# Order of the first projections in an encoder layer on one core: values of two attention units first, per token tile

## The chip, the cores and the metric

The kernel runs on one core of one Trainium2 chip. The metric is device microseconds of the whole program on that core; the time of a kernel is the median of its runs. Each engine (TensorE or PE, VectorE or DVE, ScalarE or ACT, GpSimd or POOL, SyncE or SP, which only issues transfers here) executes its own instructions strictly in program order and waits on semaphores where the kernel says so.

## What is computed

One layer of an encoder over 512 tokens of width 1024, in float32: a normalised input, one wide projection into queries, keys and values of three kinds of attention, the attentions, a gated mix, and a feed-forward part. The change touches only the first lines:

```python
u = rmsnorm(h, g_pre_mix[i])
proj = u @ w_in[i]
qa, ka, va, qb, kb, vb, qc, kc, vc = jnp.split(proj, SPLIT_POINTS, axis=-1)
...
ya = diff_attention(qa..., ka..., va..., t5_table[:, :A_HEADS], lam, lam_init, subln_g[i])
```

## The kernel before, in words

Every float32 product is done as three products of parts: an operand is split into a high part (a cast copy, by ACT) and a low part (the source less the high part, by DVE for activations, by POOL for weights), and `triple` multiplies high by high, high by low and low by high into the same bank of PSUM. The normalised and transposed input lies in `u_hi` and `u_lo` (128 features x 8 x 512 tokens). Weights come in tiles of 128 columns (1024 x 128), in a ring of `RING` = 4 slots: SP loads a tile into `raw`, ACT casts it into `whi` (`w_hi`, L1014), POOL makes `wlo` in four pieces (`w_lo`, L856), and then the tile is ready for PE.

The order of the projections is written out in `attention_gemms`. It gives a list of tiles (`TILES`: q, k and v of unit 0, then q, k and v of each next unit, and tiles of the gate late), and a list of steps (`STEPS`: one step is one k of one tile, three matmuls of 512 columns). Attention has 12 units (four of kind A, four C, four B) of four slots each (one for 128 queries); `STEPS[-1]` is the head, before the first slot, and `STEPS[s]` are the steps that PE does in slot s, while ACT and DVE work on the softmax. In a slot PE does its steps, then `pv(s - 1)`, `qk(s + 1)` and `turn_probs(s)` (transposes of the probabilities). `FINISH[t]` is the slot in which a tile is complete. A finished q or k tile is taken out of its bank in two stages: ACT copies the high part (`proj_out`; L1066 for q, L1075 for k), then DVE makes the low part (`proj_low`; L1641 for q, L1647 for k). A v tile has features on the partitions, so ACT copies it to `v_feat` (L1086), PE turns it back in four transposes at the unit's first slot (`turn_v`, L2376), ACT copies the high part (L1178) and DVE makes the low part (L1824). `bank_free` holds PE back before a tile until the bank's former tile is out.

The head, in order. The input comes in four token tiles x(0) to x(3). ACT sums the squares (`square`, L1024), POOL makes the reciprocal root (`rstd`, L866), DVE scales (L1581 in halves for tiles 0 and 1, L1563 for tiles 2 and 3), PE transposes (L2320, L2299), ACT copies the high part (L1041, L1028), DVE makes the low part (L1587, L1569). A matmul of ones (L2313) spreads the gain over the partitions. `keep_clock_up` issues transposes of the identity that compute nothing (L2307). Then PE multiplies q and k of unit 0 over token tiles 0 and 1 (weights stationary, 256 columns), with tiles 2 and 3 of the input transposed between and the small tables turned by `turn_tables` (L2288 to L2293), then over tiles 2 and 3, then v of unit 0 over all 512 tokens, and then `qk(0)` (L2364, L2365), which waits until q and k of unit 0 are out (`proj_lo`). DVE meanwhile runs `tables()` (L1597 to L1621): it copies the turned tables, makes the bias by distance in 29 copies, and waits for the mask. After it DVE takes up `proj_low` of the first tiles, in order of tiles. ACT stores the bias table to DRAM, from which SP loads the bias of each head.

Of the kernel before, what the change touches and what calls it, by code (L numbers as in the profile page):

```python
# [41 lines left out]
SLOT_CUTS = {"A": (0, 5, 11, 17, 24), "C": (0, 5, 10, 16, 24), "B": (0, 6, 11, 17, 24)}  # L42
WARM_UP = (14, 2, 6)
# [79 lines left out]
def attention_gemms():  # L123


    tiles, steps = [], {-1: []}
    for kind in "qkv":
        steps[-1] += [(len(tiles), k) for k in range(KT)]
        tiles.append((kind, 0))
    gate = 0  # L130
    for u in range(UNITS):
        mine = []
        if u + 1 <= 8:
            mine = [("q", u + 1), ("k", u + 1), ("v", u + 1)]
            if u + 1 == 8:
                mine[:2] = mine[1::-1]
        elif u + 1 < UNITS:
            mine = [("gate", gate), ("q", u + 1), ("gate", gate + 1)]
            gate += 2
        else:  # L140
            mine = [("gate", gate), ("gate", gate + 1)]
        flat = [(len(tiles) + i, k) for i in range(len(mine)) for k in range(KT)]
        tiles += mine
        cuts = SLOT_CUTS[branch(u)] if len(flat) == 3 * KT else [len(flat) * qt // TT for qt in range(TT + 1)]
        for qt in range(TT):
            steps[4 * u + qt] = flat[cuts[qt]:cuts[qt + 1]]
    finish = {t: s for s, st in steps.items() for t, k in st if k == KT - 1}
    return tiles, steps, finish
# [6 lines left out]
def split_slot(t):  # L155

    return -1 if t < RING else FINISH[t - RING] + 1
# [15 lines left out]
def build_encoder(nc, x, w_in, lambda_q1, lambda_k1, lambda_q2, lambda_k2, subln_g, t5_table, sinks,  # L173
# [16 lines left out]
    with ExitStack() as ctx:  # L190
# [67 lines left out]
        def turned_tokens(t, done):  # L258


            return bank2(TT - 1 - t if done == 0 else t).rearrange("p (k n) -> p k n", n=P)

        def first_turned(part):

            return bank2(TT - 1 - part).rearrange("p (k n) -> p k n", n=2 * P)
# [199 lines left out]
        small_loaded = [sem(f"small_loaded{i}") for i in range(9)]  # L465
# [9 lines left out]
        first_half_hi = sem("first_half_hi")  # L475
        quarter_lo = sem("quarter_lo")
        xs_first = sem("xs_first")
        tile_used = sem("tile_used")
# [154 lines left out]
        def _(sp):  # L633
# [5 lines left out]
            load_x(2)  # L639

            def load_small():
# [3 lines left out]
                sp.dma_start(conv_in[:, 3, :], conv_b[0].rearrange("(j n) -> j n", n=P)).then_inc(small_loaded[4], 16)  # L645
                sp.dma_start(bgate_in, b_gate[0].rearrange("(j n) -> j n", n=P)).then_inc(small_loaded[5], 16)
                for i, v in enumerate((lambda_q1, lambda_k1, lambda_q2, lambda_k2)):
                    sp.dma_start(lam_in[:, i, :], v[0].partition_broadcast(P)).then_inc(small_loaded[7], 16)
                sp.dma_start(sink[:], sinks[0].partition_broadcast(P)).then_inc(small_loaded[6], 16)
                sp.dma_start(sub_raw[:], subln_g[0].rearrange("(n a) -> n a", a=1)).then_inc(small_loaded[8], 16)  # L650
# [10 lines left out]
            def by_k(t, r, src, n=KT):  # L661

                h = n // 2
                load(t, r, (raw_k[:, r, 0:h, :], raw_k[:, r, h:n, :]), (src[:, 0:h, :], src[:, h:n, :]))

# [31 lines left out]
            for u in range(4, UNITS - 1):  # L697
                bias_before[min(t for t in range(2 * RING, T_ATT) if split_slot(t - RING) >= TT * (u - 1))] = u
            for t, (kind, n) in enumerate(TILES):
# [7 lines left out]
                if t == 1:  # L707
                    load_x(3)
# [4 lines left out]
                if kind == "gate":  # L713
                    by_k(t, t % RING, gate_v[:, :, n, :])
                else:
# [3 lines left out]
                    by_k(t, t % RING, win_v[:, :, col:col + P])  # L719
            load_biases(UNITS - 1)  # L720
# [122 lines left out]
        def _(pool):  # L843
# [34 lines left out]
            def w_lo_quarter(t, i):  # L878
                c = slice(256 * i, 256 * (i + 1))
                pool.tensor_tensor(wlo[:, t, c], raw[:, t, c], whi[:, t, c].bitcast(F32), ALU.subtract)\  # L880
                    .then_inc(quarter_lo if i < 3 else w_lo_done, 1)

            rstd(0, 0)
            rstd(0, 1)
            rstd(0, 2)
            pool.wait_ge(first_half_hi, 1)
            w_lo_quarter(0, 0)
            w_lo_quarter(0, 1)
            pool.wait_ge(w_hi_done, 1)
            w_lo_quarter(0, 2)  # L890
            w_lo_quarter(0, 3)
            rstd(0, 3)
            pool.wait_ge(w_hi_done, 2)
            for i in range(4):
                w_lo_quarter(1, i)
# [6 lines left out]
            pool.wait_ge(mask_done, 1)  # L902
            for s in range(SLOTS):
# [106 lines left out]
        def _(act):  # L1010
# [5 lines left out]
            def w_hi_at(t):  # L1016
                if t >= RING:
                    act.wait_ge(tile_used, t - RING + 1)
# [17 lines left out]
            act.wait_ge(x_loaded[2], 16)  # L1036
            square(0, 2, x_tok[:, 2, :])

            def u_high_first(part):
                act.wait_ge(xs_turned, part + 1)  # L1040
                act.copy(u_hi[:, 4 * part:4 * part + 4, 0:2 * P], first_turned(part)).then_inc(u_hi_done, 1)  # L1041

            u_high_first(0)
            act.wait_ge(raw_loaded[0], 32)
            act.copy(whi[:, 0, 0:512], raw[:, 0, 0:512]).then_inc(first_half_hi, 1)
            u_high_first(1)
            act.copy(whi[:, 0, 512:1024], raw[:, 0, 512:1024]).then_inc(w_hi_done, 1)
            act.wait_ge(x_loaded[3], 16)
            square(0, 3, x_tok[:, 3, :])
# [1812 lines left out]
```

## Time and profile before

| | us |
|---|---|
| median of 3 runs | 844.48 (843.78 to 846.26) |
| the profiled execution | 843.84 |
| its span, first to last instruction | 842.0 |
| PE busy in the span | 833.5 (99%) |
| DVE busy | 653.8 (78%) |
| ACT busy | 481.5 (57%) |
| POOL busy | 400.1 (48%) |

The profile gives one execution. The span is 1.84 us shorter than that execution's own time; what lies around it is not in the trace. A PE row of the timeline lists a matmul with a modelled duration that overlaps the next one; the distance from start to start is what a matmul costs in a row of them. The granted clock is 1.00 nearly throughout.

### The profile page before, as it was taken

Reading aid. Unit: us, or ns where it says so; the run is one execution under the profiler, and the core shown is the slowest. Engines: PE = TensorE matmul, PEld = TensorE weight load, DVE = VectorE, ACT = ScalarE, POOL = GpSimd, SP = SyncE. Lnnn points to the kernel's source line nnn. Section 1 sums busy time; section 2 is a strip of 40 time slices with the busy share of each in tenths; the row PEclk is TensorE's granted clock in tenths of the full one; section 3 lists DMA queues with packets and bytes.
Section 4 is the critical chain, followed back from the end, with each engine's and each line's share of the span. In section 5 each row is a group of like instructions: output and inputs, shape, how many; then the busy total and the mean of one; then the engine's idle time right before and its main releaser. Section 6 shows DMA issues by size and latency. Waiting matters only on the chain.

```text
span 842.0 us, 13461 instructions
## 1 busy us (share of the span) xinstructions
PE 833.5 (99%) x4721; PEld 729.3 (87%) x4721; DVE 653.8 (78%) x1257; ACT 481.5 (57%) x906; POOL 400.1 (48%) x511
## 2 busy tenths in 40 slices
PE   8999999999999999999999999999999999999997
PEld 7888888888888888999998889899999999988885
DVE  6678877788866767966544389988888888999996
ACT  6566666777666664544444447456565656545662
POOL 5554443334444446987667435756565656010002
PEclk9999999999999999999999999999999999999999
DMA  8542223233233212333335641555553433396584
GB/s 229 158 121 55 64 86 99 75 98 82 83 82 81 62 41 88 113 110 110 107 101 206 198 147 51 172 175 179 162 178 112 131 110 129 132 329 219 172 285 157
DMA packets 139079, 111.35 MB, mean 132 GB/s; under 512 B 7591, under 2 KB 122223, under 8 KB 137732
## 3 DMA queue, kind: packets, MB, share of 16 engines
q1 hardware_dynamic: 137386, 102.05, 39.8%
q0 software_dynamic: 720, 5.24, 1.7%
q10 hardware_dynamic: 906, 3.20, 1.0%
q8 instruction: 38, 0.62, 0.3%
q14 instruction: 29, 0.24, 0.1%
HBM read 97.05 MB, written 13.42 MB: 131 GB/s over the span
## 4 chain that ended last, share of the span: by engine, by line
PE 94%; DVE 2%; POOL 1%; DMA 1%; ACT 1%; issue 1%; DVEq 0%; SPq 0%; ACTq 0%
PE banks L2280 23%; PE banks L2282 23%; PE banks L2281 23%; PE banks L2557 3%; PE banks L2556 3%; PE banks L2555 3%; PE banks L2456 2%; PE banks L2365 2%; PE banks L2364 2%; PE banks L2726 1%; PE banks L2725 1%; PE banks L2724 1%; PE banks L2428 1%; PE banks L2435 1%; PE banks L2419 1%; DVE scratch L1976 1%
## 5 line engine op out<-in xcount | busy, mean ns | idle before, releaser
L856 POOL TENSOR_TENSOR ring_lo<-ring_raw,ring_hi 128x256 fp32r<-128x256 f32 x376 | 307.2, 850 | 262.8 <-ACT ring_hi L1014 262.4
L2280 PE MATMUL banks<-u_hi,ring_hi 128*128 128x512 f32 (+1 forms) x612 | 231.3, 378 | 0.5 <-POOL ring_lo L880 0.5
L2282 PE MATMUL banks<-u_hi,ring_lo 128*128 128x512 f32 (+1 forms) x612 | 226.4, 370 | 0.0
L2281 PE MATMUL banks<-u_lo,ring_hi 128*128 128x512 f32 (+1 forms) x612 | 226.1, 370 | 0.0
L2282 PEld LDWEIGHTS banks<-u_hi,ring_lo 128*128 128x128 f32 x612 | 115.2, 188 | 20.2
L2280 PEld LDWEIGHTS banks<-u_hi,ring_hi 128*128 128x128 f32 x612 | 115.4, 189 | 18.6 <-DVE u_lo L1587 0.8
L2281 PEld LDWEIGHTS banks<-u_lo,ring_hi 128*128 128x128 f32 x612 | 115.6, 189 | 18.0
L1014 ACT CAST ring_hi<-ring_raw 128x1024 fp32r<-128x1024 f32 x95 | 98.9, 1044 | 37.4 <-PE banks L2282 24.1
L2101 DVE SCALAR_TENSOR_TENSOR wide<-banks,cols,wide 128x511 f32<-128x511 f32 x88 | 64.6, 745 | 3.5 <-ACT wide L1374 1.6
L2280 PE MATMUL banks<-pages,ring_hi 128*128 128x512 f32 (+1 forms) x180 | 61.2, 340 | 0.0
L2281 PE MATMUL banks<-pages,ring_hi 128*128 128x512 f32 (+1 forms) x180 | 61.2, 340 | 0.0
L2282 PE MATMUL banks<-pages,ring_lo 128*128 128x512 f32 (+1 forms) x180 | 61.1, 340 | 0.0
L863 POOL TENSOR_SCALAR norm_ms<-norm_ss 128x1 f32<-128x1 f32 x15 | 6.0, 399 | 100.0 <-ACT pages L1024 99.8
L1162 ACT ACTIVATE scratch<-scratch,negmax 128x193 f32<-128x193 f32 (+5 forms) x96 | 49.4, 517 | 6.7 <-DVE negmax L1752 6.0
L2280 PE MATMUL banks<-ring_hi,pages 128*128 128x512 f32 x112 | 44.0, 393 | 0.0
L2281 PE MATMUL banks<-ring_lo,pages 128*128 128x512 f32 x112 | 43.6, 389 | 0.0
L2282 PE MATMUL banks<-ring_hi,pages 128*128 128x512 f32 x112 | 43.6, 389 | 0.0
L940 POOL TENSOR_TENSOR ring_lo<-ring_raw,ring_hi 128x256 fp32r<-128x256 f32 x44 | 37.6, 874 | 11.7 <-ACT ring_hi L1402 11.7
L1374 ACT ACTIVATE wide<-banks,cols 128x512 f32<-128x512 f32 x40 | 31.0, 775 | 21.1 <-DVE banks L2075 13.4
L1752 DVE CUSTOM_DVE_ANT_0 scratch<-banks,scratch 128x128 f32<-128x128 f32 (+3 forms) x64 | 28.8, 487 | 13.0 <-PE banks L2456 9.1
L2282 PEld LDWEIGHTS banks<-pages,ring_lo 128*128 128x128 f32 x180 | 34.2, 190 | 3.7
L2280 PEld LDWEIGHTS banks<-pages,ring_hi 128*128 128x128 f32 x180 | 34.2, 190 | 3.6
(325 smaller groups left out, 1991.9 us busy)
## 6 DMA issues: line engine op xcount, KB each, us to landing
ring_raw<-in_w_ffn_up_dram SPq DMA_DIRECT2D x88, 256.0 KB, 3.6
ring_raw<-in_w_in_dram SPq DMA_DIRECT2D x60, 256.0 KB, 3.4
ring_raw<-in_w_ffn_down_dram SPq DMA_DIRECT2D x55, 256.0 KB, 3.6
ring_raw<-in_w_gate_dram SPq DMA_DIRECT2D x48, 256.0 KB, 3.2
split_tokens<-pages SPq DMA_DIRECT2D x5, 1024.0 KB, 7.0
pages<-split_tokens POOLq DMA_DIRECT2D x5, 1024.0 KB, 6.5
ring_raw<-in_w_out_dram SPq DMA_DIRECT2D x16, 256.0 KB, 3.1
second_tokens<-wide SPq DMA_DIRECT2D x10, 384.0 KB, 3.9
```

Source lines behind the costliest of these rows:

```text
L856: last = pool.tensor_tensor(wlo[:, r, c], raw[:, r, c], whi[:, r, c].bitcast(F32), ALU.subtract)
L940: last = pool.tensor_tensor(dst[:, c], src[:, c], hi[:, c].bitcast(F32), ALU.subtract)
L1014: act.copy(whi[:, r, :], raw[:, r, :]).then_inc(w_hi_done, 1)
L1162: act.activation(p_out, p_in, ACT.Exp, scale=-1.0, bias=negmax[:, s % 2, m:m + 1], accum_out=rowsum[:, s % 2, m:m + 1]).then_inc(exp_done, 1)
L1374: act.activation(wide[:, 4 + 2 * j + c, :], psum[:, 2 * j + c, :], ACT.Identity, scale=cols[:, 88 + fc:89 + fc], bias=cols[:, 132 + fc:133 ...
L1752: dve.tensor_tensor_reduce(scratch[:, P_PAGE + m, c0:c0 + n], psum[:, SC_BANK + m, 0:n], scratch[:, BIAS_PAGE + b % 4, j0:j0 + n], -1.0, c ...
L2101: dve.scalar_tensor_tensor(out=y[:, back:SEQ], in0=psum[:, 2 * j + c, 0:SEQ - back], scalar=tap, in1=y[:, back:SEQ], op0=ALU.mult, op1=ALU ...
L2280: pe.matmul(out, lhs_hi, rhs_hi, start=start, stop=False)
L2281: pe.matmul(out, lhs_hi, rhs_lo, start=False, stop=False)
L2282: return pe.matmul(out, lhs_lo, rhs_hi, start=False, stop=stop)
L2555: pe.matmul(dst, w_h, u_h, start=False, stop=False, skip_group_check=True)
L2556: pe.matmul(dst, w_h, u_l, start=False, stop=False, skip_group_check=True)
```

## The change

The tiles are in another order. The first two are `va0` and `vb0`: together they are the value weights of units 0 and 1 (256 columns), `va` for k 0 to 3 and `vb` for k 4 to 7. Their products are made by a new function with the tokens as the stationary operand, one token tile after the other, 256 columns moving, so that the values come out with tokens on the partitions. q0 and k0 follow, still in the head; then q1, k1, v2 in unit 0, q2, k2, v3 in unit 1, and so on. The head holds four tiles where it held three; the slots hold 272 steps where they held 280. v of units 0 and 1 is no longer turned. ACT and DVE take `va` and `vb` out of the banks in two pieces of 128 x 256 each. The head's order of token tiles, of splits and of loads changes with it; x(2) and x(3) are issued behind the first two weight tiles. The weight splits of tiles 4 and 5 are done ahead of the slots, and their casts wait until both value tiles are used. The function `first_turned` and the early turns for token tiles 0 and 1 together are gone; twelve fewer empty transposes are issued (28 to 16).

```diff
-SLOT_CUTS = {"A": (0, 5, 11, 17, 24), "C": (0, 5, 10, 16, 24), "B": (0, 6, 11, 17, 24)}
-WARM_UP = (14, 2, 6)
+GEMM_ORDER = ("va0 vb0 q0 k0 q1 k1 v2 q2 k2 v3 q3 k3 v4 q4 k4 v5 q5 k5 v6 q6 k6 v7 q7 k7 v8 k8 q8 "
+              "gate0 q9 gate1 gate2 q10 gate3 gate4 q11 gate5 gate6 gate7")
+SLOT_CUTS = ((0, 5, 11, 17, 23),) + 3 * ((0, 5, 11, 17, 24),) + 4 * ((0, 5, 10, 17, 24),) + (
+    (0, 6, 11, 17, 23), (0, 5, 11, 16, 22), (0, 5, 11, 16, 22), (0, 3, 7, 10, 14))
+SPLIT_AHEAD = RING + 2
+WARM_UP = (11, 4, 1)
...
+    steps, at = {-1: flat[:RING * KT]}, RING * KT
+    for u, cuts in enumerate(SLOT_CUTS):
...
@@ SP
             load_x(0)
             load_x(1)
-            load_x(2)
...
-                if t == 1:
+                if t == 2:
+                    load_x(2)
                     load_x(3)
...
+                elif kind in ("va", "vb"):
+                    by_k_wide(t, t, win_v[:, 4 * t:4 * t + 4, VA:VA + 2 * P])
@@ POOL
             rstd(0, 0)
             rstd(0, 1)
+            w_lo(0, 0)
+            pool.wait_ge(w_hi_done, 2)
+            w_lo_quarter(1, 0)
             rstd(0, 2)
...
+            w_lo_quarter(1, 1)
+            w_lo_quarter(1, 2)
+            w_lo_quarter(1, 3).then_inc(w_lo_done, 1)
             rstd(0, 3)
...
+            for t in range(RING, SPLIT_AHEAD):
+                w_lo(t, t % RING)
@@ ACT
             square(0, 1, x_tok[:, 1, :])
...
+            w_hi_at(0)
+            act.wait_ge(first_turned, 1)
+            act.copy(u_hi[:, 0:4, 0:P], turned_tokens(0, 0)[:, 0:4, :]).then_inc(u_first_hi, 1)
+            act.wait_ge(xs_turned, 1)
+            act.copy(u_hi[:, 4:8, 0:P], turned_tokens(0, 0)[:, 4:8, :]).then_inc(u_hi_done, 1)
+            w_hi_at(1)
+            u_high(1, 0)
             act.wait_ge(x_loaded[3], 16)
+            act.wait_ge(squares, 3)
             square(0, 3, x_tok[:, 3, :])
-            w_hi_at(1)
+            w_hi_at(2)
             u_high(2, 0)
             u_high(3, 0)
-            w_hi_at(2)
             w_hi_at(3)
...
+                elif kind in ("va", "vb"):
+                    for h in range(2):
+                        dst, half = first_values(g, 0, h)
+                        last = act.copy(dst, half)
+                    last.then_inc(proj_act, 1)
...
+            proj_out(0)
             act.wait_ge(lam_dots, 2)
             act.activation(lam_exp[:], lam_dot[:], ACT.Exp).then_inc(lam_exps, 1)
-            proj_out(0)
             proj_out(1)
+            w_hi_at(RING)
             act.wait_ge(dist_done, 2)
             act.dma_start(bias_dram[0:12, :], dist_ab).then_inc(dist_stored, 16)
             act.dma_start(bias_dram[12:20, :], dist_c).then_inc(dist_stored, 16)
+            for t in range(RING + 1, SPLIT_AHEAD):
+                w_hi_at(t)
             proj_out(2)
+            proj_out(3)
@@ DVE
+            xs(0, 1, x_tok[:, 1, :], spread_gain())
             for part in range(2):
...
+                dve.wait_ge(u_hi_done if part else u_first_hi, 1)
+                dve.tensor_tensor(u_lo[:, ks, 0:P], turned_tokens(0, 0)[:, ks, :], u_hi[:, ks, 0:P].bitcast(F32), sub)\
+                   .then_inc(u_lo_done if part else u_first_lo, 1)
+            dve.wait_ge(x_loaded[2], 16)
+            dve.tensor_tensor_reduce(tmp, x_tok[:, 2, :], x_tok[:, 2, :], 1.0, 0.0, ALU.mult, ALU.add,
+                                     norm_ss[:, 0, 2:3]).then_inc(squares, 1)
+            u_low(1, 0)
...
             tables()
-            for g in range(3):
+            for g in range(RING):
                 proj_low(g)
@@ PE
                     pe.wait_ge(proj_act, g - 1)
+                    if g <= RING:
+                        pe.wait_ge(v_lo, 2)
...
+            pe.wait_ge(u_first_hi, 1)
+            pe.wait_ge(w_hi_done, 1)
+            value_products(0, u_hi, whi, first)
+            turn_tokens(1, 0, x_tok[:, 1, :])
+            pe.wait_ge(u_first_lo, 1)
+            value_products(0, u_lo, whi, first)
+            pe.wait_ge(u_hi_done, 1)
+            pe.wait_ge(w_hi_done, 2)
+            value_products(0, u_hi, whi, second)
+            pe.wait_ge(u_lo_done, 1)
+            value_products(0, u_lo, whi, second)
+            pe.wait_ge(w_lo_done, 1)
+            value_products(0, u_hi, wlo, first)
+            pe.wait_ge(u_hi_done, 2)
+            value_products(1, u_hi, whi, both)
+            pe.wait_ge(u_lo_done, 2)
+            value_products(1, u_lo, whi, both)
+            value_products(1, u_hi, wlo, first)
+            turn_tokens(2, 0, x_tok[:, 2, :])
+            pe.wait_ge(w_lo_done, 2)
+            value_products(0, u_hi, wlo, second)
+            value_products(1, u_hi, wlo, second)
+            pe.wait_ge(u_hi_done, 3)
+            value_products(2, u_hi, whi, both)
+            turn_tokens(3, 0, x_tok[:, 3, :])
+            pe.wait_ge(u_lo_done, 3)
+            value_products(2, u_lo, whi, both)
+            value_products(2, u_hi, wlo, both).then_inc(tile_used, 1)
+            turn_tables()
+            pe.wait_ge(u_hi_done, 4)
+            value_products(3, u_hi, whi, both)
+            pe.wait_ge(u_lo_done, 4)
+            value_products(3, u_lo, whi, both)
+            value_products(3, u_hi, wlo, both).then_inc(tile_used, 1)
             gemm_steps(STEPS[-1][2 * KT:])
...
-                if qt == 0 and u <= 8:
+                if qt == 0 and 2 <= u <= 8:
                     turn_v(u)
```

## Rows read from the trace of the kernel before

**Rows 1.** The page's first part: busy time, share of the span, instructions of each engine
```profile
PE 833.5 (99%) x4721; PEld 729.3 (87%) x4721; DVE 653.8 (78%) x1257; ACT 481.5 (57%) x906; POOL 400.1 (48%) x511
```
**Rows 2.** Waits of PE, whole span: engine, line, releaser; total us, times, longest
```profile
PE banks L2280 <- POOL ring_lo L880: 0.5, 1, 0.5
PE banks L2299 <- DVE scratch L1563: 0.3, 1, 0.3
```
**Rows 3.** Timeline of the head: start, duration, engine, line, operation, [idle before, releaser]
```profile
6.95 0.75 DVE L1581 SCALAR_TENSOR_TENSOR scratch<-scratch,norm_rstd,banks 128x512 f32<-128x512 f32 x1 [2.51 <-POOL norm_rstd L866]
...
7.75 0.66 PE L2320 MATMUL banks<-ident,scratch 128*128 128x128 f32 x4
...
11.99 0.36 PE L2280 MATMUL banks<-u_hi,ring_hi 128*128 128x256 f32 x1 [0.55 <-POOL ring_lo L880]
...
14.94 1.03 PE L2299 MATMUL banks<-ident,scratch 128*128 128x128 f32 x8
...
18.02 0.19 PE L2288 MATMUL banks<-ident,wide 32*12 32x32 f32 x1
...
19.05 0.39 PE L2280 MATMUL banks<-u_hi,ring_hi 128*128 128x256 f32 x1
```
**Rows 4.** Timeline of the head: PE at the end of k and of v of unit 0
```profile
27.06 0.40 PE L2280 MATMUL banks<-u_hi,ring_hi 128*128 128x512 f32 x1
...
32.53 0.22 PE L2364 MATMUL banks<-pages 128*128 128x128 f32 x1
```
**Rows 5.** Transfers that SP issued at 1.7 and at 2.6 us: us to landing
```profile
scratch<-in_x_dram SPq DMA_DIRECT2D x1, 512.0 KB, 6.1
...
ring_raw<-in_w_in_dram SPq DMA_DIRECT2D x1, 256.0 KB, 7.0
```
**Rows 6.** Timeline: prices of the pieces that the new head issues
```profile
11.12 2.88 POOL L880 TENSOR_TENSOR ring_lo<-ring_raw,ring_hi 128x256 fp32r<-128x256 f32 x4 [1.23 <-ACT ring_hi L1045]
...
13.13 1.27 DVE L1563 SCALAR_TENSOR_TENSOR scratch<-scratch,norm_rstd,banks 128x1024 f32<-128x1024 f32 x1
...
13.42 1.05 ACT L1014 CAST ring_hi<-ring_raw 128x1024 fp32r<-128x1024 f32 x1
...
37.03 0.59 ACT L1178 CAST pages<-banks 128x512 fp32r<-128x512 f32 x1 [1.23 <-PE banks L2376]
...
37.65 0.69 DVE L1824 TENSOR_TENSOR pages<-banks,pages 128x512 fp32r<-128x512 f32 x1 [1.89 <-ACT pages L1178]
```
**Rows 7.** Timeline of DVE: first and last instruction of `tables()` (36 rows in all)
```profile
19.60 0.17 DVE L1597 COPY tab_ab<-banks 12x32 f32<-12x32 f32 x1
...
27.01 0.16 DVE L1621 TENSOR_SCALAR neg_sink<-sink 128x8 f32<-128x8 f32 x1
```
**Rows 8.** Timeline: k of unit 0 taken out of its bank
```profile
27.26 0.58 ACT L1075 CAST pages<-banks 64x512 fp32r<-64x512 f32 x1 [0.46 <-PE banks L2282]
...
28.63 1.39 DVE L1647 TENSOR_TENSOR pages<-banks,pages 64x512 fp32r<-64x512 f32 x2
```
**Rows 9.** Timeline of PE: the turn of v of unit 0, and what follows it
```profile
36.39 0.60 PE L2376 MATMUL banks<-ident,v_feat 128*128 128x128 f32 x4
36.75 0.36 PE L2364 MATMUL banks<-pages 128*128 128x256 f32 x1
```
**Rows 10.** Timeline of slots in the last unit: probabilities out, then `pv` (L2435)
```profile
286.32 0.75 ACT L1114 CAST pages<-banks 128x256 fp32r<-128x256 f32 x2 [0.64 <-PE banks L2456]
...
294.89 0.85 DVE L1673 TENSOR_TENSOR pages<-banks,pages 128x256 fp32r<-128x256 f32 x2
...
296.62 0.64 PE L2435 MATMUL banks<-pages 128*128 128x256 f32 x4
```
**Rows 11.** Stretches near the end of the program: length, busy (x) by engine, granted clock, DMA
```profile
838.00:839.00 1.00, 0.00 (x0) 0.00 (x0) 0.91 (x3) 0.00 (x0) 0.00 (x0) 1.00 0.97 397
...
840.00:841.00 1.00, 0.00 (x0) 0.00 (x0) 0.00 (x0) 0.00 (x0) 0.00 (x0) 0.50 1.03 383
```
**Rows 12.** Timeline of PE: its last matmul
```profile
835.74 0.39 PE L2726 MATMUL banks<-ring_hi,pages 128*128 128x512 f32 x1
```

More of the change, by code:

```diff
@@ L123, in attention_gemms @@
 def attention_gemms():
[L126 to L144, printed above, removed]
+    tiles = []
+    for word in GEMM_ORDER.split():
+        kind = word.rstrip("0123456789")
+        tiles.append((kind, int(word[len(kind):])))
+    flat = [(g, k) for g in range(len(tiles)) for k in range(KT)]
+    steps, at = {-1: flat[:RING * KT]}, RING * KT
+    for u, cuts in enumerate(SLOT_CUTS):
         for qt in range(TT):
-            steps[4 * u + qt] = flat[cuts[qt]:cuts[qt + 1]]
+            steps[4 * u + qt] = flat[at + cuts[qt]:at + cuts[qt + 1]]
+        at += cuts[TT]
     finish = {t: s for s, st in steps.items() for t, k in st if k == KT - 1}
@@ L464, in build_encoder @@
         x_loaded = [sem(f"x_loaded{t}") for t in range(TT)]
-        small_loaded = [sem(f"small_loaded{i}") for i in range(9)]
+        small_loaded = [sem(f"small_loaded{i}") for i in range(7)]
         raw_loaded = [sem(f"raw_loaded{r}") for r in range(RING)]
@@ L697, in _ @@
             for u in range(4, UNITS - 1):
-                bias_before[min(t for t in range(2 * RING, T_ATT) if split_slot(t - RING) >= TT * (u - 1))] = u
+                later = [t for t in range(2 * RING, T_ATT) if split_slot(t - RING) >= TT * (u - 1)]
+                bias_before[min(later, default=T_ATT)] = u
             for t, (kind, n) in enumerate(TILES):
@@ L1180, in _ @@
                     w_hi_at(t)
-                for g in range(3, T_ATT):
+                for g in range(RING, T_ATT):
                     if FINISH[g] == s and (TILES[g][0] == "q" and u >= 8):
@@ L1185, in _ @@
                     y_high(s - 1)
-                for g in range(3, T_ATT):
+                for g in range(RING, T_ATT):
                     if FINISH[g] == s and not (TILES[g][0] == "q" and u >= 8):
@@ L1628, in proj_low @@
                 src = psum[:, proj_bank(g), :]
+                if kind in ("va", "vb"):
+                    dve.wait_ge(proj_act, g + 1)
+                    for h in range(2):
+                        lo, half = first_values(g, 1, h)
+                        last = dve.tensor_tensor(lo, half, first_values(g, 0, h)[0].bitcast(F32), sub)
+                    last.then_inc(v_lo, 1)
+                    return
                 if kind not in "qk":
@@ L1801, in projections @@
             def projections(s):
-                for g in range(3, T_ATT):
+                for g in range(RING, T_ATT):
                     if FINISH[g] == s and not projection_low_at_once(g):
@@ L1826, in _ @@
                     y_low_a(u - 1)
-                for g in range(3, T_ATT):
+                for g in range(RING, T_ATT):
                     if FINISH[g] == s and projection_low_at_once(g):
@@ L2395, in pv @@
                 if qt == 0 and u <= 8:
-                    pe.wait_ge(v_lo, u + 1)
+                    pe.wait_ge(v_lo, max(u + 1, 2))
                 vh = v_page(u, 0)
@@ new lines, in _ @@
+            first, second, both = range(4), range(4, KT), range(KT)
+            pe.wait_ge(u_first_hi, 1)
[9 more added lines that the diff above has]
+            value_products(0, u_lo, whi, second)
@@ L2496, in _ @@
                 gemm_steps(first_steps)
-                if qt == 0 and u <= 8:
+                if qt == 0 and 2 <= u <= 8:
                     turn_v(u)
```

133 lines of the change are left out of this document (50 added, 83 removed).

## The prediction

> **What bounds the kernel now.** I read the busy times first: PE is busy 99% of the span, the next engine 78% [rows 1]. Then the waits of PE: over 842 us it waits 0.5 us for a low part of the first weights at 12 us and 0.3 us for a scaled token tile at 16 us, and between 16 and 470 us for nothing [rows 2]. So PE's own order of work is the path. An instruction less on PE is worth its distance to the next one, a wait added on PE costs its whole length, and what DVE, ACT and POOL do counts only where PE comes to stand for it. Last I read the head in order of time, for the work that has to end before the first product at 11.99 us [rows 3]; and the places at which PE passes from one part to the next [rows 3, 4].
>
> **Prices.** A product of 256 columns costs 0.121 us: from 19.05 to 27.06 us there are 66 of them [rows 3, 4]. One of 512 costs 0.228 us: v of unit 0 is 24 of them from 27.06 to 32.53 us, so a tile is 5.47 us [rows 4]. Eight transposes of a token tile are about 0.95 us with the change of kind at both ends (the row says 1.03, its end is modelled), and the tables 1.03 us [rows 3]. A weight cast is 1.05 us, a weight's low part 2.88 us in four pieces of 0.72, a cast of 128 x 512 from a bank 0.59, its low part on DVE 0.69, a scaling of 128 x 1024 on DVE 1.27 us [rows 6].
>
> **The start of the products, a gain.** The work on PE is the same (96 products of 256 columns in place of 96, and one full tile more in the head is one less in the slots). What moves is the moment at which PE can begin. The new order needs x(0) alone. DVE's first scaling stays at 6.95, PE's first four transposes at 7.75 to 8.4, the other four follow by 9.15 [rows 3]. ACT must cast the first weight tile before it copies the turned tokens. That tile is now third in SP's queue, where x(2) was. x(2) landed at 1.7 + 6.1 = 7.8 us, the second half of the first weight tile at 2.6 + 7.0 = 9.6 [rows 5]: these are the bounds for it. I take 7.9, since the same number of bytes stands ahead of it as ahead of x(2). Then cast to 8.95, copy of the first half to 9.6, first product at 9.65: 2.35 us sooner than 11.99.
>
> From there PE has 96 x 0.121 = 11.6 us of products, three token tiles to turn (2.85) and the tables (1.03): 15.5 us if nothing is late. Is anything late? By the same prices: ACT casts the second weight tile 10.2 to 11.25, u_high(1) to 12.3; DVE makes the low parts of tile 0 by 11.0, squares x(2) by 12.3 (x(2) has now two weight tiles ahead of it, as x(3) nearly had, about 11 us), low part of tile 1 by 13.6, wanted at 14.0; POOL, whose `rstd` of tiles 2 and 3 now stands behind one and behind three more pieces, has w_lo(0) at 12.0, rstd(2) at 13.5, w_lo(1) at 15.8, rstd(3) at 16.6; DVE scales tile 2 by 14.9 (wanted at 15.5) and tile 3 by 17.9 (wanted at 18.6). Each is ahead of PE by 0.4 to 0.8 us. I add 0.2 us for seams: the values end at 25.4 us. Before, the same 96 products ended at 27.06 [rows 4]. Gain 1.65 us.
>
> **The turns that go.** v of units 0 and 1 needs no `turn_v`: twice 0.36 us on PE (36.39 to 36.75) [rows 9]. Gain 0.7 us. The twelve empty transposes fewer lie ahead of the first product, where PE waits anyway: nothing.
>
> **A hold at k0, a loss.** `bank_free(3)` makes PE wait, before k of unit 0, for `v_lo` = 2: both value tiles out of their banks. The low parts are on DVE, behind all of `tables()`, and q of unit 0 is PE's only cover. Let the tables be turned at T (about 22.5 us). PE then has 24 products and a full tile: T + 2.9 + 5.5 = T + 8.4. DVE has `tables()`, 19.60 to 27.17, 7.6 us [rows 7], and four subtractions of 128 x 256, 0.43 each [rows 10], with handovers T + 9.5. Loss 1.1 us. It doesn't depend on when the head starts. If DVE is 1.1 us quicker the hold is nil; if ACT's turn at `proj_out(1)` came late it would be more, but that is due at 26.5 us and wanted at 31. Queued behind the waiting PE is everything.
>
> **A hold at `qk(0)`, a loss.** `qk(0)` waits until k of unit 0 has both parts. Before, v of unit 0 lay between k and `qk(0)`, 5.47 us, while k was out at 30.0 us: hidden. Now k is the last tile of the head and PE's next instruction is `qk(0)`; the steps of slot 0 stand behind it. The whole way out lies open: 0.2 us from PE's last k product to ACT's start (27.06 to 27.26), two casts of 0.58, then DVE's two subtractions, 28.63 to 30.02 [rows 4, 8]: 27.06 to 30.02 is 2.96; DVE was 0.1 late there, so 2.9 us. Loss 2.9 us. It could be less only if ACT or DVE were quicker at the same instructions.
>
> **What is late next.** ACT now casts tiles 4 and 5 ahead of q's way out, so q of unit 0 (done 31.0) is out near 35 us, still ahead of k. After `qk(0)` nothing is late: the bias table is stored some 3 us later than before, since the tables are turned later, but `qk(0)` itself comes at about 40.5 us, 8 us later; and w_lo(4), for q1, is done near 30.5. In the slots each v tile ends one step into the next unit, which moves an ACT copy by a slot. The thinnest cover is in unit 11, with 3, 4, 3 and 4 steps where there were four each. There ACT and DVE bring the probabilities out [rows 10]; the low part ended at 295.74 for a `pv` at 296.62: 0.88 us. A step is 0.68, so 0.2 us is left. I put it at zero, and at most 0.7 us in each of the two slots.
>
> **Sum.** -1.65 - 0.7 + 1.1 + 2.9 = +1.65 us. The profiled span of 842.0 becomes 843.65, the profiled execution's 843.84 becomes 845.5. The median of the three runs is 0.6 above that execution, so the forecast for the median is 844.48 + 1.6 = 846.1. A measurement of this kernel can tell about 0.3%, 2.5 us, from no change: the likeliest answer is no difference, with a sign towards slower.
>
> **A clock that falls.** PE's last product begins at 835.74 [rows 12], it works no more, and the granted clock is 0.50, which is 1.2 GHz, from 840 us on [rows 11]; until 839 it was 1.00. That is over 3 us of rest at full clock, more than the 2.9 us of the hold at `qk(0)`. So by the rows the clock holds. The Trainium skill, "TensorE: Matmul & The Clock Gate", section "HAM oscillation — how this bites in real kernels", says that rests between bursts of matmuls can put the array back to half its clock; it speaks against this change, and by it the rival below would come true.
>
> **Rivals.**
> - The holds are not there, or are covered (for instance because DVE reaches the low parts of the values sooner and k's way out is mostly hidden). Then only the gains are left, -2.35 us: 842.1. Against it stands the order on PE, in which nothing lies between k0 and `qk(0)`. With only the first hold gone it is 845.0, in my range.
> - On the other side, slower: the first weight tile lands late. ACT is in order, so its cast holds back the copy of the turned tokens and with it the first product. Landing at 9.6 [rows 5] puts the first product at 11.35 and the sum at +3.35: 847.8. It decides (over 2.5 us in all) from a landing at about 8.8 us. For it: the tile's rows are shorter than those of x. Against it: as many bytes ahead as x(2) had.
> - The clock falls in the hold at `qk(0)` and PE runs at half its rate afterwards. Running the about 3 us after it at half rate loses 1.5 us, a whole slot 0 about 4 us: 847.6 to 850, taken as 848.8. It decides from a rest as long as the one at the end.
> - The lighter slots lose their cover: 0.7 us in unit 11's two and as much again in units 9 and 10: up to +2.8, taken as +1.4: 847.5.
>
> **How the numbers follow.** My forecast has 0.68, the holds covered 0.07, late weights 0.10, the falling clock 0.08, the slots 0.07. The unknown sizes are the landing (7.4 to 9.6), DVE's 9.5 us of work at the first hold, and the seams: -1.0 to +1.2 about the forecast, 845.1 to 847.3. To hold the time 8 times in 10 the range reaches to late weights and part of the way to the covered holds: 844.2 to 848.4. Faster by over 0.3% (below 841.9): 0.03. Slower by over 0.3% (above 847.0): a tenth of my own case and most of the three slow rivals, 0.26. The rest, 0.71, is within 0.3%.
>
> **What would show it.** In the profile of after: the first product (line of `value_products`) at 9.65 us; the first of the 512-column products at 25.4; before k's first product PE waits for DVE about 1.1 us; before `qk(0)` PE waits for DVE 2.7 to 2.9 us; the waits of PE in total some 5 us in place of 0.8 after 12 us; only 28 transposes on the line of `turn_v` where there were 36; the granted clock 1.00 throughout; no wait of PE in 45 to 312 us. The forecast is wrong if PE has something to do between k0 and `qk(0)`, if the first product comes later than 10.5 us, or if PE waits in the slots.

## The result and the profile after

| | before | after |
|---|---|---|
| median of 20 executions each | 844.07 us (843.22 to 846.96) | 846.79 us (844.82 to 851.33) |
| profiled execution | 843.84 us, span 842.0 | 847.32 us, span 845.5 |

The ratio is 1.0034, 95% interval [1.0022, 1.0046]: 2.7 us slower. The forecast was 846.1. The two medians differ by more than the interval allows for chance, and the executions of after are spread over 6.5 us where those of before are spread over 3.7. That wider spread is followed up below.

Busy time per engine, first part of the page of after, against [rows 1]:
```profile
PE 833.3 (99%) x4701; PEld 728.2 (86%) x4701; DVE 651.2 (77%) x1261; ACT 478.9 (57%) x904; POOL 399.9 (47%) x511
```
PE is busy for 0.2 us less and the span is 3.5 us longer, so PE stands still for longer. (Its busy time also holds what a lower clock adds and what the turns that are gone take off; both come below.) Waits of PE in after (engine, line, releaser; total us, times, longest), against [rows 2]:
```profile
PE banks L2382 <- DVE pages L1666: 2.8, 1, 2.8
PE banks L2326 <- POOL ident L853: 1.5, 1, 1.5
PE banks L2484 <- ACT u_hi L1042: 1.3, 1, 1.3
PE banks L2484 <- POOL ring_lo L862: 0.3, 1, 0.3
PE banks L2453 <- DVE pages L1692: 0.2, 1, 0.2
PE banks L2484 <- ACT u_hi L1032: 0.2, 1, 0.2
```
The first row is the hold at `qk(0)` (a hold is a wait of PE that nothing covers). There is no row for a hold of k of unit 0 behind the low parts of the values (it would name L2299 and DVE L1645): that hold isn't there. The rest lies ahead of or in the value phase, except for 0.2 us at L2453.

Timeline of the head of after (start, duration, engine, line, operation, idle before and releaser), against [rows 3, 4, 6]:
```profile
8.46 1.04 ACT L1018 CAST ring_hi<-ring_raw 128x1024 fp32r<-128x1024 f32 x1 [1.67 <-DMA ring_raw<-in_w_in_dram]
...
9.58 3.79 POOL L862 TENSOR_TENSOR ring_lo<-ring_raw,ring_hi 128x256 fp32r<-128x256 f32 x4 [1.88 <-ACT ring_hi L1018]
...
10.04 0.74 PE L2484 MATMUL banks<-ring_hi,u_hi 128*128 128x256 f32 x4 [1.33 <-ACT u_hi L1042]
...
11.22 1.55 DVE L1597 CUSTOM_DVE_ANT_0 wide<-scratch 128x1024 f32<-128x1024 f32 x1
...
13.42 0.74 PE L2484 MATMUL banks<-ring_lo,u_hi 128*128 128x256 f32 x4 [0.34 <-POOL ring_lo L862]
...
26.58 0.40 PE L2299 MATMUL banks<-u_hi,ring_hi 128*128 128x512 f32 x1
```
The first product comes at 10.04 instead of 11.99, the values end at 26.58 instead of 27.06. So 1.95 us of earlier start leave only 0.48 at the end of the phase. The low part of the first weight tile takes 3.79 us where the same four pieces took 2.88 before.

Timeline of the passage from k to `qk(0)` in after:
```profile
37.26 0.39 PE L2301 MATMUL banks<-u_hi,ring_lo 128*128 128x512 f32 x1
...
37.69 1.17 ACT L1074 CAST pages<-banks 64x512 fp32r<-64x512 f32 x2 [3.02 <-PE banks L2301]
...
38.89 1.39 DVE L1666 TENSOR_TENSOR pages<-banks,pages 64x512 fp32r<-64x512 f32 x2 [3.49 <-ACT pages L1074]
...
40.43 0.30 PE L2382 MATMUL banks<-pages 128*128 128x128 f32 x1 [2.78 <-DVE pages L1666]
```
It is the chain that the prediction wrote down: two casts, two subtractions, and PE with nothing to do.

Stretches of half a microsecond around it (length, busy and number for PE, PEld, DVE, ACT and POOL, then the granted clock of TensorE, DMA share, GB/s):
```profile
40.00:40.50 0.50, 0.07 (x1) 0.10 (x1) 0.28 (x1) 0.00 (x0) 0.00 (x0) 1.00 1.15 346
40.50:41.00 0.50, 0.50 (x4) 0.50 (x4) 0.06 (x1) 0.00 (x0) 0.00 (x0) 0.63 1.20 312
41.00:41.50 0.50, 0.50 (x3) 0.50 (x3) 0.37 (x3) 0.23 (x1) 0.00 (x0) 0.50 1.18 287
...
43.50:44.00 0.50, 0.50 (x3) 0.40 (x2) 0.00 (x0) 0.50 (x1) 0.50 (x2) 0.50 0.00 0
44.00:44.50 0.50, 0.50 (x3) 0.42 (x3) 0.00 (x0) 0.08 (x1) 0.50 (x1) 0.96 0.06 16
```
After the wait of 2.8 us, when `qk(0)` has just begun, the clock falls to its lower level, 1.2 GHz, and stays there for some 3.5 us of full work. Products of 512 columns follow each other there at 0.43 us instead of 0.23:
```profile
42.08 0.63 PE L2301 MATMUL banks<-u_hi,ring_lo 128*128 128x512 f32 x1
42.51 0.63 PE L2299 MATMUL banks<-u_hi,ring_hi 128*128 128x512 f32 x1
```
The account of the profiled execution is this. Before, `qk(0)` stood at 32.53 [rows 4] behind three tiles; after has four tiles ahead of it, so equal work would put it one tile of 5.47 us later, at 38.00. It stands at 40.43: +2.43 (2.8 to 2.9 of hold, 0.5 of gain in the values). The half clock adds about +1.7 over `qk(0)` and slot 0. The two turns that are gone give -0.7. That is +3.4 of the span's +3.5. It is one execution against one.

### The profile page after: what moved, and what is told of

The parts are those of the page before. It is cut to its first block, busy times and chain, and to the rows that moved or that the text cites. A ratio compares the mean times of both kernels' runs of the same rounds, so it can differ in the third digit from the quotient of the medians.

```text
span 845.5 us, 13419 instructions
## 1 busy us (share of the span) xinstructions
PE 833.3 (99%) x4701; PEld 728.2 (86%) x4701; DVE 651.2 (77%) x1261; ACT 478.9 (57%) x904; POOL 399.9 (47%) x511
## 4 chain that ended last, share of the span: by engine, by line
PE 96%; DVE 2%; DMA 1%; ACT 1%; POOL 0%; issue 0%; SPq 0%; DVEq 0%
PE banks L2299 24%; PE banks L2301 24%; PE banks L2300 24%; PE banks L2598 3%; PE banks L2599 3%; PE banks L2600 3%; PE banks L2474 2%; PE banks L2382 2%; PE banks L2383 2%; PE banks L2769 1%; PE banks L2768 1%; PE banks L2767 1%; PE banks L2446 1%; PE banks L2484 1%; PE banks L2453 1%; DMA ring_raw<-in_w_in_dram 1%
## 5 line engine op out<-in xcount | busy, mean ns | idle before, releaser
L862 POOL TENSOR_TENSOR ring_lo<-ring_raw,ring_hi 128x256 fp32r<-128x256 f32 x380 | 311.2, 851 | 283.4 <-ACT ring_hi L1018 283.1
L2299 PE MATMUL banks<-u_hi,ring_hi 128*128 128x512 f32 (+1 forms) x580 | 222.7, 384 | 0.0
L2301 PE MATMUL banks<-u_hi,ring_lo 128*128 128x512 f32 (+1 forms) x580 | 217.9, 376 | 0.0
L2300 PE MATMUL banks<-u_lo,ring_hi 128*128 128x512 f32 (+1 forms) x580 | 217.6, 375 | 0.0
L2301 PEld LDWEIGHTS banks<-u_hi,ring_lo 128*128 128x128 f32 x580 | 109.4, 189 | 20.2
L2300 PEld LDWEIGHTS banks<-u_lo,ring_hi 128*128 128x128 f32 x580 | 109.9, 189 | 18.1
L2299 PEld LDWEIGHTS banks<-u_hi,ring_hi 128*128 128x128 f32 x580 | 109.7, 189 | 17.9
L2299 PE MATMUL banks<-pages,ring_hi 128*128 128x512 f32 (+1 forms) x180 | 61.2, 340 | 0.0
L2299 PE MATMUL banks<-ring_hi,pages 128*128 128x512 f32 x112 | 44.0, 393 | 0.0
L944 POOL TENSOR_TENSOR ring_lo<-ring_raw,ring_hi 128x256 fp32r<-128x256 f32 x44 | 37.2, 864 | 11.7 <-ACT ring_hi L1409 11.7
L1118 ACT CAST pages<-banks 128x256 fp32r<-128x256 f32 (+5 forms) x32 | 17.9, 561 | 35.9 <-PE banks L2474 35.5
```

The source lines that it names most:

```text
L862: last = pool.tensor_tensor(wlo[:, r, c], raw[:, r, c], whi[:, r, c].bitcast(F32), ALU.subtract)
L944: last = pool.tensor_tensor(dst[:, c], src[:, c], hi[:, c].bitcast(F32), ALU.subtract)
L2299: pe.matmul(out, lhs_hi, rhs_hi, start=start, stop=False)
L2300: pe.matmul(out, lhs_hi, rhs_lo, start=False, stop=False)
L2301: return pe.matmul(out, lhs_lo, rhs_hi, start=False, stop=stop)
```

## The experiments

My theory after this reading: the hold at `qk(0)` costs 2.8 us by its length and, in most executions, the clock's fall on top of it; the rest of the change is a gain of about 1.5 us. The rivals: the clock's fall belongs to this one execution; or the loss sits elsewhere (the lighter slots, the head). A second question was why the hold at k0 did not come and the value phase ran long.

**The kernel after, once more.** No edit.

> The changed kernel as it is, timed on the chip on which the next three run. Theory (hold and clock): PE stands 2.8 us before qk(0), and the granted clock falls to 0.5 there for some 3.4 us in most executions; 1.0034 of the kernel before, with a wider spread than before has. A rival, that the loss lies in the slots, would show waits of PE between 46 and 312 us.

Measured: 847.85 us (845.06 to 848.14, 7 executions), before 843.89, ratio 1.0033 [1.0022, 1.0045]. By luck its profiled execution was the fastest of the seven: span 843.3, mean granted clock 0.999. One of its waits of PE:
```profile
PE banks L2382 <- DVE pages L1666: 2.8, 1, 2.8
```
and two stretches, with the columns as above:
```profile
40.00:41.00 1.00, 1.00 (x7) 0.86 (x7) 0.52 (x4) 0.58 (x3) 0.00 (x0) 1.00 1.16 305
41.00:42.00 1.00, 1.00 (x6) 0.81 (x5) 0.59 (x3) 1.00 (x3) 0.00 (x0) 1.00 0.37 93
```
The same wait of 2.8 us, and the clock stays at 1.00. So the hold comes every time, the fall doesn't. Each execution's mean granted clock is recorded, so all 27 executions of this kernel can be sorted by it. Four have 0.998 or more: 844.8 to 845.6 us. The other 23 have 0.997 or less: median 847.3, 846.2 to 851.3. Of 84 executions of the kernel before on three chips none is below 0.998. A clock below 0.998 therefore belongs to this kernel and comes in most of its executions, and by the medians (845.1 against 847.3) those executions are about 2 us longer. That the place is the hold at `qk(0)` is seen in the profile above; the mean alone doesn't say where the clock fell. Nor are the 23 alike: on this chip two stand at 846.2 us (0.996 and 0.997) and four at 847.9 to 848.1 (0.995). A fall of 3.5 us takes 0.002 off the mean, so those at 0.995 seem to have had more time at the lower clock than the profile shows; none of them was profiled, and where they had it is open.

**The hold filled.** Five steps of q of unit 1 are done ahead of `qk(0)` and taken from unit 0's slots.
```diff
+AHEAD_STEPS = 5
-SLOT_CUTS = ((0, 5, 11, 17, 23),) + ...
+SLOT_CUTS = ((0, 5, 9, 13, 18),) + ...
-    steps, at = {-1: flat[:RING * KT]}, RING * KT
+    steps, at = {-1: flat[:RING * KT + AHEAD_STEPS]}, RING * KT + AHEAD_STEPS
```


> The first five steps of q1 (15 products, 3.4 us) are done before qk(0) and not after it; unit 0 then has 5, 4, 4 and 5 steps in its slots. Hold-and-clock theory: they cover the 2.8 us of k0's way out, the clock stays at 1.00, and 4.5 us come back against the changed kernel: about 1.8 us faster than before, ratio 0.998, less what the lighter slots 1 to 3 of unit 0 lose (slot 3 had 1.1 us of cover with seven steps; up to 0.5 us). Rival (the loss is in the value phase or the slots): no more than 1 us comes back, ratio 1.002 or more.

Measured: 843.65 us (843.3 to 845.93, 11 executions), ratio 0.9993 [0.9984, 1.0003], all clocks 0.998 or more. With real work in the hold, 4.2 us of after's 847.85 on the same chip are gone, more than the whole loss of 4.0. The hold is where the loss was. Two new waits took a part back:
```profile
PE banks L2475 <- DVE scratch L1789: 0.6, 2, 0.4
...
PE banks L2438 <- DVE pages L1688: 0.4, 1, 0.4
```

**The hold kept, the array kept busy.** Nine products that nobody reads between k0 and `qk(0)`; the time that PE loses to the hold stays.
```diff
+            for _ in range(9):
+                pe.matmul(psum[:, O_BANK, :], whi_k[:, 3, 0, :], u_hi[:, 0, :], start=True, stop=True)
             pe.wait_ge(q_lo_cleared, 2)
             qk(0)
```


> Adds nine products of 512 columns that nobody reads, between the last product of k0 and qk(0): 2.05 us of work inside a hold of 2.8. The hold stays. Theory that the clock falls because PE stands still: clock 1.00 from 37 us on, slot 0 is 1.7 us shorter, the median 1.5 to 2 us below the changed kernel, ratio to before about 1.001, and the spread of the runs becomes that of before. Rival (the fall has nothing to do with the hold): clock and time as in the changed kernel.

Measured: 845.16 us (844.82 to 846.92, 11 executions), ratio 1.0015 [1.0006, 1.0023]. All clocks 0.998 or more. PE's timeline:
```profile
36.79 2.20 PE L2534 MATMUL banks<-u_hi,ring_hi 128*128 128x512 f32 x9
39.74 0.30 PE L2382 MATMUL banks<-pages 128*128 128x128 f32 x1 [0.74 <-DVE pages L1666]
```
and the stretch behind it:
```profile
41.00:42.00 1.00, 1.00 (x6) 0.82 (x5) 0.49 (x3) 1.00 (x4) 0.00 (x0) 1.00 0.20 53
```
`qk(0)` comes no sooner, yet the kernel is 2.7 us faster than after on its chip, and lands on the four executions of after whose clock did not fall. This splits the loss: the wait itself leaves 845.16 - 843.89 = +1.3 us for the whole change, the clock adds 2.7 on this chip (1.7 by the first comparison's medians, 846.8 against some 845.1). The two differ as the share of long executions does: four of seven here have 0.995, and four of twenty there.

**The same with 19 empty transposes** in place of the products (`keep_clock_up(19)`).

> As the one with nine products, but with 19 empty transposes of 128 x 128 instead (2.05 us at 0.108 each). If transposes keep the clock as products do: same time as that one. The Trainium skill, page TensorE: Matmul & The Clock Gate, Part 4, says that the full clock doesn't engage for transposes, as they don't count as busy in the same way: by it the clock falls as in the changed kernel, and the time is 1.5 to 2 us above the one with products.

Measured: 845.55 us (844.92 to 848.38, 12 executions), ratio 1.0018 [1.0009, 1.0027]; no execution has a clock below 0.998. PE's timeline:
```profile
37.22 2.23 PE L2326 MATMUL banks<-ident 128*128 128x128 f32 x19
40.16 0.30 PE L2382 MATMUL banks<-pages 128*128 128x128 f32 x1 [0.70 <-DVE pages L1666]
```
and the stretch in which `qk(0)` starts:
```profile
40.00:41.00 1.00, 0.84 (x6) 0.83 (x7) 0.40 (x4) 0.06 (x1) 0.00 (x0) 1.00 0.93 261
```
Transposes held the clock as products did. The Trainium skill, "TensorE: Matmul & The Clock Gate", "Part 4: PE-mode transpose", says that the full clock doesn't engage for transposes; whether they could raise it no run here shows, but they kept it.

**Why the hold at k0 was absent.** DVE's 29 small copies in `tables()` took 4.99 us before and 2.45 in after (2.80 in its second profile, where the first 0.7 us of them still ran beside POOL). In before POOL was making low parts beside them; in after it stood idle from 25.9 to 28.5 us. The kernel before, with POOL held back until the copies are done:
```diff
             for t in range(2, RING):
+                if t == 3:
+                    pool.wait_ge(dist_done, 2)
                 w_lo(t, t)
```


> The kernel before, with one wait more: POOL makes the low part of the fourth weight tile only after DVE has ended its 29 table copies. Theory that the copies are slow because POOL works beside them (4.99 us in the kernel before with POOL busy, 2.45 us in the changed kernel with POOL at rest): the 29 copies take about 2.5 us, `tables()` ends near 24.8 us and not 27.2. Rival (the copies' price depends on something else in the order, such as ACT or PE): they stay near 5 us. Either way the time stays within 0.3 us of before, since neither is on PE's path.

Measured, one execution: 844.12 us, before 844.01. Timelines of DVE and POOL, first before, then this kernel:
```profile
19.45 5.77 POOL L856 TENSOR_TENSOR ring_lo<-ring_raw,ring_hi 128x256 fp32r<-128x256 f32 x8 [1.77 <-ACT ring_hi L1014]
...
21.59 4.99 DVE L1609 COPY wide<-tab_ab 12x421 f32<-12x421 f32 x29
```
```profile
22.16 2.24 DVE L1611 COPY wide<-tab_ab 12x421 f32<-12x421 f32 x29
...
24.67 2.83 POOL L856 TENSOR_TENSOR ring_lo<-ring_raw,ring_hi 128x256 fp32r<-128x256 f32 x4 [2.53 <-DVE wide L1614]
```
The same copies take less than half the time once POOL is quiet. POOL itself lost little to them. This is the duration of its eight pieces before (min/median/max in ns); in other stretches the median is 728 to 748:
```profile
L856 POOL TENSOR_TENSOR ring_lo<-ring_raw,ring_hi x8: 733/738/890, 19.4 to 24.5; 128x256 fp32r<-128x256 f32 x8
```

**Why the first weight's low part took 3.8 us.** In after, DVE's squares of x(2) (1.55 us) run beside it. The squares go to ACT:
```diff
             u_high(1, 0)
+            act.wait_ge(x_loaded[2], 16)
+            square(0, 2, x_tok[:, 2, :])
             act.wait_ge(x_loaded[3], 16)
-            act.wait_ge(squares, 3)
...
-            dve.wait_ge(x_loaded[2], 16)
-            dve.tensor_tensor_reduce(tmp, x_tok[:, 2, :], x_tok[:, 2, :], 1.0, 0.0, ALU.mult, ALU.add,
-                                     norm_ss[:, 0, 2:3]).then_inc(squares, 1)
```


> The changed kernel, with the squares of x(2) on ACT behind u_high(1) and not on DVE. Theory that DVE's 1.55 us pass over two SBUF operands slowed POOL's w_lo(0) (3.79 us for the four pieces where 2.88 were priced): w_lo(0) is back near 2.9 us, PE's wait for it (0.3 to 0.4 us) is gone, and the values end about 0.5 us sooner. Rival (it was the ten twenty-fifths of other DVE work, the low parts that read a bank): w_lo(0) stays at 3.5 us or more. The time still carries the hold and the clock.

Measured: 846.35 us (846.07 to 847.54, 9 executions), ratio 1.0027 [1.0017, 1.0036]. POOL's timeline:
```profile
8.67 2.81 POOL L862 TENSOR_TENSOR ring_lo<-ring_raw,ring_hi 128x256 fp32r<-128x256 f32 x4 [0.71 <-ACT ring_hi L1018]
```
and in after, the durations of the four pieces (min/median/max in ns):
```profile
L862 POOL TENSOR_TENSOR ring_lo<-ring_raw,ring_hi x4: 726/733/1713, 9.6 to 11.7; 128x256 fp32r<-128x256 f32 x4
```
One piece of the four took 1.71 us, the others 0.73: the one beside the squares. With them gone PE's wait for POOL is gone too. The hold and the fallen clock stay (PE waits 2.8 us in the profiled execution, the clock is at 0.50 from 40.0 to 43.0 us, and eight of nine executions have 0.997 or less), and with them most of the loss. The ninth has 0.998 and the longest time of the nine, 847.54: in a single execution a mean of 0.998 is no proof that the clock held, so 23 of 27 above is a lower bound.

**Five steps ahead, fewer in the first slot.** As the first filling, cuts (0, 3, 8, 13, 18), meant to remove its waits.

> As e1_fill5, five steps of q1 ahead of qk(0), but unit 0 has 3, 5, 5 and 5 steps in its slots in place of 5, 4, 4 and 5. The waits of PE in unit 0 (0.36 for the low part in slot 1, 0.42 and 0.15 for probabilities) should go, since slot 0 had 1.9 us to spare and slots 1 and 2 had none: 0.8 us less than e1_fill5, ratio to before 0.998. Rival: the waits only move to slot 0, and the time stays.

Measured: 844.37 us (844.03 to 845.01, 11 executions), ratio 1.0001 [0.9992, 1.001], so no better than the first filling. I had expected less waiting and got more: 1.0 us for the low part of the first probabilities. ACT's timeline shows why:
```profile
43.24 2.42 ACT L1066 ACTIVATE pages<-banks 64x512 fp32r<-64x512 f32 x4
45.68 0.27 ACT L1119 CAST pages<-banks 128x128 fp32r<-128x128 f32 x1
```
q of unit 1 is finished within slot 0, and its way out, four operations on an engine that works in order, stands ahead of the high part of slot 0's probabilities. The first filling had q of unit 1 end in slot 0 too.

**Four steps ahead**, cuts (0, 3, 8, 13, 19): q of unit 1 finishes in slot 1.

> Four steps ahead of qk(0), 2.73 us of work for a hold of 2.8, and 3, 5, 5 and 6 steps in the slots of unit 0. If the fill has only to be as long as k0's way out, PE waits 0.1 us before qk(0), the clock stays at 1.00, and the time is that of e6_fill5_late within 0.2 us; slot 3 keeps all its cover.

Measured: 842.41 us (841.92 to 844.83, 10 executions), ratio 0.9977 [0.9966, 0.9989]: faster than both kernels. PE no longer waits ahead of `qk(0)` nor in unit 0, and ACT's order is turned round:
```profile
43.77 0.27 ACT L1119 CAST pages<-banks 128x128 fp32r<-128x128 f32 x1
45.07 2.41 ACT L1066 ACTIVATE pages<-banks 64x512 fp32r<-64x512 f32 x4
```

**Is it the number of steps, or the slot in which q of unit 1 (q1) ends?** Five steps as in the two fillings above, but with cuts (0, 2, 7, 12, 18), which also end q1 in slot 1.

> Five steps of q1 stand ahead of q(0), as in e1 and e6, but the last four steps of q1 stand in the second slot of unit 0, not the first, so that q1's way out (ScalarE, some 2.4 us for its four copies) comes behind the first exponentials' low parts and not ahead of them. By the theory that in e6 this way out made the products wait for probs low (1.0 us at the longest), that wait goes, although five steps are ahead as there; the first slot, with two steps, may wait some 0.2 us. Ratio about 0.998, as e7. By the rival, that five steps ahead leave unit 0 too few to cover its slots wherever they stand, waits of about 1 us remain in unit 0 and the ratio is about 1.000, as e6.

Measured: 842.57 us (842.12 to 845.43, 12 executions), ratio 0.9975 [0.9962, 0.9987]. (The text above speaks of the last four steps; against the filling before it, it is one step that left slot 0, the eighth and last of q1.) No wait for the probabilities is left; behind the head PE waits once, for 0.2 us, a wait that all these kernels have. The slot in which q1 ends decides, not the number of steps ahead: one step less in slot 0 took off 1.8 us (on another chip; by the ratios 2.2). The step went to slot 3, which the edit couldn't avoid; of the filling before, 1.5 us of PE's waits stood in slot 1, behind q1's way out, and 0.15 in slot 3.

**Four steps ahead with the squares on ACT.**

> e7 with the squares of x(2) on ScalarE, as in e5. By the theory that VectorE's operation of 1.55 us slows GpSimd's low part of the first weight tile (3.8 us beside it, 2.8 without), the low part takes 2.8 us, PE's wait for it goes, and the kernel is some 0.3 to 0.5 us faster than e7 on the same chip: ratio about 0.997. By the rival, the head's gain is eaten by ScalarE's longer queue (the square delays the next weight tiles' casts), and the kernel stands as e7 does, within 0.2 us.

Measured: 842.53 us (841.6 to 845.34, 12 executions), ratio 0.9975 [0.9962, 0.9989], beside 842.40 without the edit. The profiled head is faster (the values end at 25.43 us, without the edit at 26.18; 0.4 of that is an earlier first product, which moves from one execution to the next in any case), the median isn't. The five fastest executions, 841.6 to 842.0, lie below nearly all of the other kernel's, but seven lie above 842.1. The profiled one lost its gain late in the program, in a wait that the profile of the kernel without the edit doesn't have:
```profile
PE banks L2766 <- ACT banks L1550: 1.2, 1, 1.2
```
It isn't the edit's own: the profile of five steps ahead with cuts (0, 3, 8, 13, 18) has the same wait, of 0.8 us. Every kernel here, before included (up to 847.4 at a full clock), has some executions 2 to 3 us above its median. Whether this wait is what parts them is open.

**Four steps ahead once more**, beside the last two.

> e7 once more, beside e8 and e9 on their chip: four steps of q1 ahead of q(0), cuts 0, 3, 8, 13, 19. If e7's gain was no accident of its chip, the ratio is again 0.997 to 0.999, with no wait of PE ahead of q(0) and the clock at 1.00 between 37 and 45 us; if it was one, the ratio is 1.000 or above.

Measured: 842.40 us (841.98 to 844.59, 12 executions), ratio 0.9973 [0.9961, 0.9985]. On a second chip the gain is the same, about 1.7 us against before.

## Why the prediction came out as it did

The number was close, 846.1 for 846.8, and in part by luck: errors of both signs met. Step by step:

- **Start of the products**: forecast 9.65 us. Measured 10.04 in the profiled execution and 9.23 in the next one; over the nine profiled executions with this head (this kernel's and those of the kernels that differ only behind it) it lies between 8.86 and 10.04. It follows the landing of the first weight tile, which the forecast put at 7.9 and the profile at about 8.4. Right within its bounds; the rival of late weights (from 8.8) did not come about.
- **The value phase** was priced at 15.75 us from the first product to the first of 512 columns and took 16.54 (16.53 to 16.57 in all nine). I had POOL's low part at 2.88 us from a row in which DVE did nothing against it; beside the squares it was 3.79, and PE waited 0.3. It also waited 0.2 for ACT. What remains, 0.5 us by subtraction, I put down to the seams between groups of four and eight products, for which I had 0.2 in all; no run tests that. With the squares on ACT the phase took 16.24 in both profiles that have them there, so beside POOL they cost 0.3. Gain at the end of the phase 0.5 and 1.3 us in the two profiles of this kernel (0.5 to 1.6 over the nine, 1.2 in the middle), forecast 1.65: this term was too large, by the length of the phase and not by its start.
- **The turns that go**: L2394 has 28 transposes, as forecast.
```profile
L2394 PE MATMUL banks<-ident,v_feat 128*128 128x128 f32 x28 | 4.2, 272 | 0.0
```
- **The hold at k0**, forecast 1.1 us, did not exist. PE came to k at 32.05, 8.4 us after the turn of the tables ended (23.7), exactly as priced. DVE was done 6.3 us after it and not 9.5:
```profile
23.72 0.18 DVE L1609 COPY tab_ab<-banks 12x32 f32<-12x32 f32 x1 [0.78 <-PE banks L2312]
...
25.53 2.45 DVE L1621 COPY wide<-tab_ab 12x421 f32<-12x421 f32 x29
...
28.61 1.42 DVE L1645 TENSOR_TENSOR pages<-banks,pages 128x256 fp32r<-128x256 f32 x4
```
  The step that failed is the transfer of `tables()` at 7.6 us from [rows 7]. I priced work on DVE by a row and didn't ask what POOL did beside it in that row, nor whether it would do so in the new order. The change moved the same low parts elsewhere, and 2.5 us went with them.
- **The hold at `qk(0)`**, forecast 2.7 to 2.9, measured 2.78 in both profiles. Rows of the trace of before gave this to 0.1 us: the two casts took 1.17 us where two of 0.58 were priced, the two subtractions 1.39 in both kernels.
- **No wait in 45 to 312 us**: one of 0.2. The slots with less work stayed covered (the rival had 1.4); it did not come about.
- **The clock**: here I was wrong. I read [rows 11, 12] as saying that PE may rest for over 3 us at full clock, and gave the fall 0.08. It came in at least 23 of 27 executions, after a rest shorter than the one at the end of the program. The failing step is the inference from a single rest in a single execution to a bound on rests of that length; the second profile, with the same 2.8 us and no fall, shows that executions differ, so one row could decide it neither way. The end of the program says the same. PE's last product starts at 835.74 in before [rows 12] and 3.5 us later, at 839.23, in after. The stretch in which the clock falls, first in before, then in after, comes only 3 us later, and its mean is lower (0.88 for 0.94):
```profile
839.00:840.00 1.00, 0.00 (x0) 0.00 (x0) 0.55 (x1) 0.00 (x0) 0.00 (x0) 0.94 0.24 90
```
```profile
842.00:843.00 1.00, 0.00 (x0) 0.00 (x0) 1.00 (x2) 0.00 (x0) 0.00 (x0) 0.88 0.47 188
```
  So at one and the same place two executions kept the full clock for different times after PE's last product. The Trainium skill, "TensorE: Matmul & The Clock Gate", section "HAM oscillation — how this bites in real kernels", says that rests between bursts of matmuls can put the array back to half its clock; the profiled execution of after agrees (0.50 behind a rest of 2.8 us), the second one doesn't (1.00 behind the same rest).

With the sizes as measured the sum is: start and turns about -1.6 (the filled kernel, 842.4 against 844.0), the hold +2.7 (845.2 against 842.4), the clock +1.6 or more (846.8 against 845.2). Together that is +2.7. The forecast of the time also started from 844.48, the median of three executions, 0.4 above the median of twenty. The forecast of +1.65 had -2.35 for the first, 0.75 too good, and +2.9 for the second, 0.2 too much; it counted a hold of 1.1 that wasn't there and left out the clock, which is larger. Had either of the last two been right alone, the number would have missed by more than it did. The comparison of 842.4 and 845.2 is across chips; before stood at 843.9 to 844.1 on all of them. The rival "holds covered", worked out at 842.1, comes close to what this reordering is worth once its hold is filled.

## To carry to other kernels

When an engine that sets the time gets a new place where nothing is queued between a product and its own consumer, write down that chain from rows, and fill the place with steps from later before judging the reordering: here 2.8 us of hold, and the clock that fell with it, hid a gain of 1.6. When you fill it, look at whose way out the moved steps bring forward on the in-order engines; the slot in which they finish mattered more than their number. And a duration from a row holds only with its neighbours: before a price is carried over, ask what ran beside it.

## What the runs showed of the hardware

- DVE and POOL can slow each other. Twenty-nine small copies from on-chip memory took 4.99 us beside POOL's subtractions, 2.24 alone, while POOL's pieces kept a median of 0.74; a piece of POOL's subtraction took 1.71 us beside a DVE product of two equal operands and 0.73 without it. The Trainium skill, "SBUF — State Buffer", section "Who interferes with whom", says that copies can take a pair of ports that DVE shares with GpSimd, and that a DVE instruction with two inputs from that memory contends with GpSimd's reads; these runs agree (4.99 against 2.24 us, 1.71 against 0.73).
- TensorE's granted clock went to its lower level after a rest of 2.8 us in two profiles (after, and after with the squares on ACT), by the mean clock in at least 23 of 27 executions of after, but not in its second profile, and stayed there for some 3.5 us of full work. After rests of 0.7 us, with products or with empty transposes ahead of them, the mean clock was 0.998 or more in all 23 executions.
